# Attention-map scores contracted over 128 rows in a two-block transformer kernel, and FFN semaphores shared

## The reference

```python
h = rms_norm_2(x, norm_mix_pre_g[l])
proj = h @ w_in[l]
mq, mk, mv, dq, dk, dv, ga, gb = jnp.split(proj, split_at, axis=-1)
...
ya = moba_attention(moba_heads(mq), moba_heads(mk), moba_heads(mv), moba_slopes)
...
yb = diff_attention(dq[:, :, 0], dq[:, :, 1], dk[:, :, 0], dk[:, :, 1], dv, lam, diff_slopes)
...
def probs(q, k):
    qc = lax.dynamic_slice_in_dim(q, t0, QB, axis=2)
    logits = jnp.einsum('bhqd,bhkd->bhqk', qc, k).astype(jnp.float32) * scale + bias[None]
    return jax.nn.softmax(jnp.where(causal, logits, NEG), axis=-1)
a = probs(q1, k1) - lam * probs(q2, k2)
return jnp.einsum('bhqk,bhke->bhqe', a.astype(v.dtype), v)
```

## Time and profile before

| | |
|---|---|
| time, median of 3 runs | 1957.36 us (1955.51 to 1958.13) |
| the profiled execution's own time | 1958.78 us |
| its span, first to last instruction | 1957.1 us |
| TensorE matmul busy | 1916.0 us, 98% of the span |
| VectorE busy | 908.2 us, 46% |
| ScalarE busy | 705.5 us, 36% |
| GpSimd busy | 176.8 us, 9% |
| mean granted TensorE clock | 0.991 of full speed |
| read from HBM | 172.67 MB, 89 GB/s over the span |

### The profile page before, as it was taken

One profiled execution on the slowest core, in us unless ns is written; L12 is line 12 of the kernel. 1 busy time (PEld: TensorE's weight loads), 2 busy tenths in 40 slices (PEclk: granted clock), 3 DMA queues, 4 the chain that ended last, 5 costly groups with the idle time before them and its releaser, 6 DMA issues.

```text
span 1957.1 us, 24117 instructions
## 1 busy us (share of the span) xinstructions
PE 1916.0 (98%) x9630; PEld 1559.2 (80%) x9630; DVE 908.2 (46%) x1182; ACT 705.5 (36%) x957; POOL 176.8 (9%) x150
## 2 busy tenths in 40 slices
PE   8999999998999999999999999999999989999998
PEld 6888888887778898888888878777667868888887
DVE  6444432447685654644443246343546454444313
ACT  5222221354534443522222143334545453222212
POOL 2000000205330200200000032000000030000000
PEclk9999999999999999999999999999999989999999
DMA  5333322232214223333322222111212323333222
GB/s 162 97 96 97 96 97 94 99 108 66 66 44 151 86 87 108 86 104 89 103 90 104 89 89 87 65 65 44 69 61 86 94 57 93 101 92 101 90 104 75
DMA packets 213697, 175.79 MB, mean 90 GB/s; under 512 B 6565, under 2 KB 201210, under 8 KB 213626
## 3 DMA queue, kind: packets, MB, share of 16 engines
q1 hardware_dynamic: 212928, 174.74, 29.1%
q10 hardware_dynamic: 698, 0.05, 0.0%
HBM read 172.67 MB, written 2.10 MB: 89 GB/s over the span
## 4 chain that ended last, share of the span: by engine, by line
PE 88%; DVE 5%; ACT 3%; POOL 2%; issue 1%; DMA 1%; SPq 0%; DVEq 0%; POOLq 0%; ACTq 0%
PE bank L484 25%; PE bank L486 24%; PE bank L485 24%; PE bank L658 6%; PE bank L531 2%; PE bank L951 1%; PE bank L532 1%; PE bank L533 1%; ACT w_hi L1049 1%; PE bank L920 1%; DVE w_lo L1511 1%; DMA w_raw<-in_w_in 1%; PE bank L935 1%; DVE n_lo L1520 1%; POOL sum_squares L425 0%
## 5 line engine op out<-in xcount | busy, mean ns | idle before, releaser
L484 PE MATMUL bank<-n_hi,w_hi 128*128 128x512 f32 x1760 | 707.9, 402 | 18.0 <-DVE n_lo L1520 9.5
L1511 DVE TENSOR_TENSOR w_lo<-w_raw,w_hi 128x2048 fp32r<-128x2048 f32 x160 | 369.1, 2307 | 744.4 <-ACT w_hi L1049 744.3
L486 PE MATMUL bank<-n_hi,w_lo 128*128 128x512 f32 x1760 | 690.9, 393 | 0.0
L485 PE MATMUL bank<-n_lo,w_hi 128*128 128x512 f32 x1760 | 690.5, 392 | 0.0
L1049 ACT CAST w_hi<-w_raw 128x2048 fp32r<-128x2048 f32 x160 | 305.4, 1909 | 600.9 <-PE bank L486 519.0
L484 PEld LDWEIGHTS bank<-n_hi,w_hi 128*128 128x128 f32 x1760 | 333.4, 189 | 103.4 <-issue 24.0
L486 PEld LDWEIGHTS bank<-n_hi,w_lo 128*128 128x128 f32 x1760 | 333.2, 189 | 71.1
L485 PEld LDWEIGHTS bank<-n_lo,w_hi 128*128 128x128 f32 x1760 | 333.8, 190 | 68.2 <-issue 2.6
L425 POOL TENSOR_TENSOR sum_squares<-sum_squares,sq 128x512 f32<-128x512 f32 x42 | 65.9, 1569 | 927.4 <-ACT sq L1064 923.0
L484 PE MATMUL bank<-h_hi,w_hi 128*128 (+1 forms) x352 | 137.1, 390 | 0.2
L486 PE MATMUL bank<-h_hi,w_lo 128*128 (+1 forms) x352 | 136.9, 389 | 0.0
(11 more groups left out here) (306 smaller groups left out, 1953.7 us busy)
## 6 DMA issues: line engine op xcount, KB each, us to landing
w_raw<-in_w_in SPq DMA_DIRECT2D x68, 512.0 KB, 4.6
w_raw<-in_ffn_gate SPq DMA_DIRECT2D x44, 512.0 KB, 4.1
w_raw<-in_ffn_up SPq DMA_DIRECT2D x44, 512.0 KB, 5.2
w_raw<-in_ffn_down SPq DMA_DIRECT2D x44, 512.0 KB, 3.9
w_raw<-in_w_gate SPq DMA_DIRECT2D x22, 512.0 KB, 4.1
w_raw<-in_w_up SPq DMA_DIRECT2D x22, 512.0 KB, 5.2
w_raw<-in_w_down SPq DMA_DIRECT2D x22, 512.0 KB, 4.2
w_raw<-in_w_kv_mem SPq DMA_DIRECT2D x16, 512.0 KB, 4.4
```

What stands on the lines that cost most here:

```text
L484: pe.matmul(acc, w_hi, x_hi, start=start, stop=False)
L485: pe.matmul(acc, w_hi, x_lo, start=False, stop=False)
L486: return pe.matmul(acc, w_lo, x_hi, start=False, stop=stop)
L1511: dve.tensor_tensor(wlo[par][:, :], raw[par][:, :], whi[par][:, :].bitcast(F32), ALU.subtract).then_inc(w_lo_ready, 1)
```

## The change

1. The columns of `w_in_2` come in the order q, k, q, k for both kinds of attention, so that units 0 and 1 hold all that maps 0 to 3 need (`MIX2_COLS`, and the destinations in VectorE's turns).
2. For each map SyncE copies the 64 rows of its k and of its q inside SBUF, each twice, into the two halves of a 128-row tile (`map_kk`, `map_qq`; four transfers of 64 x 512 float32, 128 KB each; `load_pair`). The two pairs of tiles lie on the buffers `sq` and `tmp`.
3. ScalarE rounds both tiles to float32r (`pair_split`: `map_kk_hi`, and `map_q_hi_lo`, whose two halves then both hold the high part of q). VectorE subtracts: the low part of the doubled k (`map_kk_lo`), and the low part of q into the lower half of `map_q_hi_lo` alone (`pair_lo`).
4. A part of the scores is then two float32r matmuls over 128 rows, for all 16 maps: `map_q_hi_lo` by `map_kk_hi` (high q by high k plus low q by high k in one pass) and `map_q_hi_lo` by `map_kk_lo`. The eight high and eight low parts of the moba q and k, made in turns 0 to 3 before (L1426, L1976), are gone.
5. The 18 semaphores of the three FFNs become 6; the waits count on from one FFN to the next. In the second and third FFN the waits on them are the same waits with larger numbers.

```diff
-MIX2_COLS = [256 * j for j in range(MIX2_UNITS)]
+MIX2_COLS = [256 * j for j in (0, 2, 1, 3, 4, 5, 6, 8, 7, 9)] + [256 * j for j in range(10, MIX2_UNITS)]
...
+        sq_at = cursor[0]
         sq = [sb(f"sq{s}", [P, T], F32) for s in range(2)]
         tmp = [sb(f"tmp{s}", [P, T], F32) for s in range(2)]
+        kdup = [at(f"map_kk{s}", [P, T], F32, sq_at + 2048 * s) for s in range(2)]
+        kdl = [at(f"map_kk_lo{s}", [P, T], F32R, sq_at + 2048 * s) for s in range(2)]
+        qdup = [at(f"map_qq{s}", [P, T], F32, sq_at + 4096 + 2048 * s) for s in range(2)]
...
-        mql = at("moba_q_lo", [P, HEADS, T], F32R, arena + 16 * KB)
-        mkl = at("moba_k_lo", [P, HEADS, T], F32R, arena + 48 * KB)
-        mqh = at("moba_q_hi", [P, HEADS, T], F32R, arena)
-        mkh = at("moba_k_hi", [P, HEADS, T], F32R, arena + 8 * KB)
+        kdh = at("map_kk_hi", [P, T], F32R, arena + 92 * KB)
+        qst = at("map_q_hi_lo", [P, T], F32R, arena + 94 * KB)
...
-        ffn = [{k: sem(f"{k}_{f}") for k in ("gu_scaled", "silu_ready", "h_product", "h_hi_ready", "h_ready", "down_done")}
-               for f in range(3)]
+        gu_scaled, silu_ready, h_product = sem("gu_scaled"), sem("silu_ready"), sem("h_product")
+        h_hi_ready, h_ready, down_done = sem("h_hi_ready"), sem("h_ready"), sem("down_done")
...
+            def load_pair(m):
+
+                c, rows = (m % 8) // 2, slice(64 * (m % 2), 64 * (m % 2) + 64)
+                sp.wait_ge(m2_dve, 4 + 4 * (c // 2) + (8 if m >= 8 else 0))
+                if m >= 2:
+                    sp.wait_ge(map_scores, 4 * (m - 1))
+                for dst, src in ((kdup, mk if m < 8 else dk), (qdup, mq if m < 8 else dq)):
+                    for half in range(2):
+                        sp.dma_start(dst[m % 2][64 * half:64 * half + 64, :], src[rows, c, :]).then_inc(pair_loaded[m % 2], 16)
...
+                if j >= 5:
+                    load_pair(j - 5)
...
+                if MIX2_UNITS + j - 5 < MAPS:
+                    load_pair(MIX2_UNITS + j - 5)
...
-                s_ = ffn[f]
+                h0 = FC * f
...
-                        pe.wait_ge(s_["gu_scaled"], 2 * (j - 1))
+                        pe.wait_ge(gu_scaled, 2 * (j + (h0 - 1)))
...
-                c, rows = (m % 8) // 2, slice(64 * (m % 2), 64 * (m % 2) + 64)
                 if part == 0:
-                    if m < 8:
-                        pe.wait_ge(moba_ready, HEADS + c + 1)
-                    else:
-                        pe.wait_ge(*m2_emptied(8 + c // 2))
+                    pe.wait_ge(pair_ready, 2 * m + 2)
...
-                    if m < 8:
-                        mm = products(out_, mqh[rows, c, t0], mql[rows, c, t0], mkh[rows, c, s0], mkl[rows, c, s0], True, True)
-                    else:
-                        mm = pe.matmul(out_, dq[rows, c, t0], dk[rows, c, s0], start=True, stop=True)
-                    mm.then_inc(map_scores, 1)
+                    pe.matmul(out_, qst[:, t0], kdh[:, s0], start=True, stop=False)
+                    pe.matmul(out_, qst[:, t0], kdl[m % 2][:, s0], start=False, stop=True).then_inc(map_scores, 1)
...
+            def pair_split(m):
+                act.wait_ge(pair_loaded[m % 2], 64 * (m // 2 + 1))
+                if m:
+                    act.wait_ge(map_scores, 4 * m)
+                act.copy(kdh[:, :], kdup[m % 2][:, :]).then_inc(pair_hi, 1)
+                act.copy(qst[:, :], qdup[m % 2][:, :]).then_inc(pair_hi, 1)
...
-                        if v < 4:
-                            ch = 2 * (v % 2) + b
-                            act.wait_ge(m2_dve, 2 * v + b + 1)
-                            act.copy((mqh if v < 2 else mkh)[:, ch, :], (mq if v < 2 else mk)[:, ch, :]).then_inc(moba_hi, 1)
...
                 if has_out(v - 5) and v - 5 >= 8:
                     map_root((v - 5 - 9) // 2)
+                if 0 <= v - 2 < MAPS:
+                    pair_split(v - 2)
                 if has_out(v - 4):
                     map_copies(v - 4)
...
+            def pair_lo(m):
+                dve.wait_ge(pair_hi, 2 * m + 1)
+                dve.tensor_tensor(kdl[m % 2][:, :], kdup[m % 2][:, :], kdh[:, :].bitcast(F32), ALU.subtract).then_inc(pair_ready, 1)
+                dve.wait_ge(pair_hi, 2 * m + 2)
+                dve.tensor_tensor(qst[64:P, :], qdup[m % 2][64:P, :], qst[64:P, :].bitcast(F32), ALU.subtract).then_inc(pair_ready, 1)
...
-                        src, ch = bank[2 * (v % 2) + b][:, :], 2 * (v % 2) + b
-                        if v in (0, 1, 6, 7):
-                            dve.scalar_tensor_tensor((mq if v < 2 else dq)[:, ch, :], src, 64.0 ** -0.5, rstd[:, :],
+                        src, ch = bank[2 * (v % 2) + b][:, :], 2 * (v % 6 // 2) + b
+                        if v in (0, 2, 6, 8):
+                            dve.scalar_tensor_tensor((mq if v < 4 else dq)[:, ch, :], src, 64.0 ** -0.5, rstd[:, :],
                                                      ALU.mult, ALU.mult).then_inc(m2_dve, 1)
-                        elif v in (2, 3, 8, 9):
+                        elif v in (1, 3, 7, 9):
                             dve.tensor_tensor((mk if v < 4 else dk)[:, ch, :], src, rstd[:, :], ALU.mult).then_inc(m2_dve, 1)
...
-                    for b in range(2):
-                        ch = 2 * (v % 2) + b
-                        lo_, full, hi_ = (mql, mq, mqh) if v < 2 else (mkl, mk, mkh)
-                        dve.wait_ge(moba_hi, 2 * v + b + 1)
-                        dve.tensor_tensor(lo_[:, ch, :], full[:, ch, :], hi_[:, ch, :].bitcast(F32), ALU.subtract).then_inc(moba_ready, 1)
...
                     map_maxima(v - 3)
+                if 0 <= v - 2 < MAPS:
+                    pair_lo(v - 2)
```

More of the change, by code:

```diff
@@ L267, in two_blocks @@
         vm_hi, vm_ready, ptx_hi = sem("vm_hi"), sem("vm_ready"), sem("ptx_hi")
-        moba_hi, moba_ready = sem("moba_hi"), sem("moba_ready")
+        pair_loaded = [sem("pair_loaded0"), sem("pair_loaded1")]
+        pair_hi, pair_ready = sem("pair_hi"), sem("pair_ready")
         m2_act, m2_dve, m2_tanh = sem("m2_act"), sem("m2_dve"), sem("m2_tanh")
@@ L1095, in ffn_steps @@
             def ffn_steps(f, base):
-                s_ = ffn[f]
+                h0 = FC * f
                 def gate_up(par, half, j, jj):
                     split(par, half)
-                    act.wait_ge(s_["gu_scaled"], 2 * j + 1)
-                    act.activation(sq[jj][:, :], sq[jj][:, :], ACT.Silu).then_inc(s_["silu_ready"], 1)
+                    act.wait_ge(gu_scaled, 2 * j + (2 * h0 + 1))
+                    act.activation(sq[jj][:, :], sq[jj][:, :], ACT.Silu).then_inc(silu_ready, 1)
                     if f == 2 and isinstance(j, int) and j == 0:
@@ L1110, in gate_up @@
                         dst = hhi[:, bass.ds(j, 1), :].rearrange("p o t -> p (o t)")
-                    act.copy(dst, tmp[jj][:, :]).then_inc(s_["h_hi_ready"], 1)
+                    act.copy(dst, tmp[jj][:, :]).then_inc(h_hi_ready, 1)
                 def copy_turned(i, dst):
@@ L1493, in _ @@
                     else:
-                        act.wait_ge(ffn[2]["down_done"], i + 1)
+                        act.wait_ge(down_done, 2 * (C - 1) + i + 1)
                     if i:
@@ L1529, in add_down @@
                     if c < C - 1:
-                        dve.wait_ge(ffn[f]["down_done"], c + 1)
+                        dve.wait_ge(down_done, (C - 1) * f + c + 1)
                     else:
@@ L1562, in gate_up @@
                     if not first:
-                        dve.wait_ge(s_["h_ready"], j - 1)
-                    dve.tensor_tensor(sq[jj][:, :], bank[2 * jj][:, :], rstd[:, :], ALU.mult).then_inc(s_["gu_scaled"], 1)
-                    dve.tensor_tensor(tmp[jj][:, :], bank[2 * jj + 1][:, :], rstd[:, :], ALU.mult).then_inc(s_["gu_scaled"], 1)
-                    dve.wait_ge(s_["silu_ready"], j + 1)
-                    dve.wait_ge(s_["gu_scaled"], 2 * j + 2)
-                    dve.tensor_tensor(tmp[jj][:, :], sq[jj][:, :], tmp[jj][:, :], ALU.mult).then_inc(s_["h_product"], 1)
-                    dve.wait_ge(s_["h_hi_ready"], j + 1)
+                        dve.wait_ge(h_ready, j + (h0 - 1))
+                    dve.tensor_tensor(sq[jj][:, :], bank[2 * jj][:, :], rstd[:, :], ALU.mult).then_inc(gu_scaled, 1)
+                    dve.tensor_tensor(tmp[jj][:, :], bank[2 * jj + 1][:, :], rstd[:, :], ALU.mult).then_inc(gu_scaled, 1)
+                    dve.wait_ge(silu_ready, j + (h0 + 1))
+                    dve.wait_ge(gu_scaled, 2 * j + (2 * h0 + 2))
+                    dve.tensor_tensor(tmp[jj][:, :], sq[jj][:, :], tmp[jj][:, :], ALU.mult).then_inc(h_product, 1)
+                    dve.wait_ge(h_hi_ready, j + (h0 + 1))
                     if isinstance(j, int):
```

17 lines of the change are left out of this document (8 added, 9 removed).

## The result

| | before | after |
|---|---|---|
| time, median | 1957.28 us (1955.51 to 1958.13, 4 runs) | 1929.27 us (1928.36 to 1930.66, 4 runs) |
| the profiled execution's own time | 1958.78 us | 1929.94 us |
| its span | 1957.1 us | 1928.2 us |

The ratio is 0.9859 with a 95% interval of 0.9842 to 0.9876: 28.0 us faster, where 23.2 were forecast. The time lies 4.9 us under the forecast and 0.2 us under the lower end of the range. Timed again beside the first experiments the changed kernel took 1931.34 us, ratio 0.9863 (0.9846 to 0.9879).

A forecast was written before the change was run, and what follows sets the result against it. TensorE, busy 293.00 of 293.00 us in the stage, was taken as the bound. A gain of 26.2 us less 3.0 us of waits gave 23.2 us, so 1934.2 us from the 1957.36 us median; range 1929.5 to 1943 us.

The forecast's parts named there:

- The price after: TensorE's score products after the change: eight float32r matmuls over 128 rows, 1.22 us a map, bounds 1.16 and 1.28.
- The price of a score part before: TensorE between dense products: three parts sum to 2.72 us in map 3, 3.00 us in map 14.
- The change of form: TensorE going to 64-row products and back: 0.3 us in each of 48 score parts, 14 us of the gain.
- The two waits: TensorE at the second transposes of units 16 and 18, behind ScalarE's casts: about 1.5 us each, 3.0 us lost.
- The transfers: Copies of q and k inside SBUF land in 5 us, needed after 12.5 to 16 us, costing TensorE nothing.
- FFN semaphores: Sharing semaphores over the three FFNs costs nothing: same waits at the same places.
- The clock: TensorE's granted clock around the third FFN's start may shift: 2 us allowed either way.
- No waits: Rival: TensorE does not wait in units 16 and 18, 1931.2 us; chance 0.12.
- more waits than two: Rival: ScalarE's turn bounds all eight differential units, each losing 1.5 us, 1943 us; chance 0.12.
- late transfers: Rival: pairs land late at ScalarE's pair_split, holding back copies and transposes, about 1995 us; chance 0.03.
- weight loads that no longer hide: Rival: each new TensorE matmul waits 0.19 us for its weight load, 24 us back, 1958 us; chance 0.02.
- the cost of going over stays: Rival: TensorE's 0.3 us per score part is not the form's, 14 us gain lost, about 1948 us; chance 0.06.

The follow-up runs named there:

- e2: Changed kernel with its two score products a tile over rows 0 to 63 only, low q by high k left out: 1945.06 us, ratio 0.9935 to before.
- e9: Changed kernel, casts behind ScalarE's first copy to map_pt; in turns 15 and 17 that copy ahead of tanh, casts behind the second copy: 1928.17 us.
- e10: As e2, but a map's three score parts made one behind the other at the third place of its unit: 1937.50 us, ratio 0.9894 to before.
- e11: Changed kernel with a map's three score parts at the third place of its unit, over 128 rows, nothing left out: 1931.54 us.
- e7: Kernel before with only the six FFN semaphores shared over the three FFNs: 1958.06 us, ratio 1.0000 to before.
- e1: Changed kernel with ScalarE's two casts of a pair behind the first copy to map_pt of its turn, not ahead: 1928.63 us, ratio 0.9851 to before.
- e3: Changed kernel with a third score product a tile over 128 rows, the first one made twice: 1938.33 us, ratio 0.9902 to before.
- e5: Changed kernel with GpSimd's product of distance and slope waiting for VectorE's low parts of the next pair: 1929.85 us, ratio 0.9855 to before.

## Why the prediction was right, and which term was too small

- **The bound.** Right. TensorE's products were the whole stage, and what was taken off them came off the kernel. VectorE's pair of subtractions, "some 1.3 us", takes 1.8 in ten maps; that was covered.
- **The price after.** Right: 1.22 us a map forecast, 1.19 to 1.24 measured. This measure too ends one product too soon, by 0.05 us a map, 0.8 in all.
- **The price of a score part before.** This is the term that was too small. The prediction measured "from the last dense start before it to the first after it, less that 0.23", and that ends one product too soon. The change of form also made the first dense product behind the part 0.1 us late: 48 x 0.1 = 4.8 us. e2 shows it (0.38 us for an excursion, where 0.3 was taken), and e9, which has no wait, gives the gain on TensorE with everything in it: (255.21 - 226.03) / 15 x 16 = 31.1 us, for 26.2 forecast.
- **The change of form.** Right in kind: "more than half of the gain". It is 18.2 of 31.1 us, forecast as 14. The products that are left out are the rest: 8 x 0.67 = 5.4 us for the moba maps, and 8 x 0.96 = 7.7 for the float32 products; the three make 31.3 us for the 31.1. The Trainium skill's rule is that a change of tiling mode drains the engine (TensorEngine Tiling (Array Packing), Key Properties). The runs agree in that the price belongs to the change of form (e2, e10 and e11); that it is a drain, no view here shows.
- **The two waits.** Right in place, number, releaser and length: units 16 and 18, ScalarE's copy to `map_pt`, 1.47 us for 1.5. In time they cost 3.4 us, not the forecast's 3.0, by e9. Of the working for unit 18, tanh was to end 0.35 us before TensorE wants the copy (1451.85 and 1452.2) and ends 0.07 behind (1427.73, and 1427.43 + 0.23 = 1427.66); casts, copy and handover were to take 1.85 us and take 1.56. The two errors nearly cancel, which is luck.
- **The transfers.** Right: 5 us taken. The landing times after the change, of the k tiles and then of the q tiles:

```profile
DMA to landing us min/median/max: 3.9/4.8/5.5
DMA to landing us min/median/max: 3.7/4.6/6.2
```

- **FFN semaphores.** Right, nothing (e7). **The clock.** Within the 2 us allowed.
- **The sum.** 31.1 - 3.4 = 27.7 us, between the two measured gains of 28.0 and 26.5 us. With the 4.8 us counted as gain the forecast would have been 1929.4. The lower end of the range, "all of the gain with the clock in its favour", took no error in the price before, as if a measured distance had none. That is why it was missed by 0.2 us; the second timing, 1931.34 us, lies inside the range.
- **The rivals.** No waits, more waits than two, late transfers and weight loads that no longer hide: none shows in the trace after, where the new products follow each other at 0.23 us. That the cost of going over stays is refuted by e2 and e11 together.

## What to carry to other kernels

An excursion of TensorE from 128-row to 64-row products and back costs 0.38 us here with two or four products in it and 0.41 with eight, so short excursions are the dear ones: stack operands to the full height, or make all products of the other form in one go. Measure what a piece of work costs from landmark to landmark a whole unit apart, not from its own first to last row, since it can make its neighbours late. And work added to an engine that is idle on the mean is free only behind what the bound engine waits for. Here the two turns without slack cost 1.7 us each; putting the casts behind the copy took 1.05 of it back (e1), putting the copy ahead of tanh the rest (e9).

## What the runs showed of the hardware beyond what was expected

- A change of form makes two products late, 0.1 us each, in a stream of products of 0.23 us: the first and the second of the new form, on the way in and again on the way out (e2, e10).
- A wait costs more than its idle time says: 1.68 us for 1.47, and 0.3 us in e3 for none shown.
- A VectorE subtraction with both inputs in SBUF takes 0.44 us longer when GpSimd starts a product of a 128x512 tile at that moment: 1.12 and 0.69 us. The Trainium skill (SBUF — State Buffer, SBUF: two separate sides) has a lock between these two engines for such a pair, held for the whole instruction of the one that starts first. The kind agrees and the length doesn't: by its record, which is rough for GpSimd, the product lasts 1.49 us, but VectorE is held up only until about 0.46 us after its start (three distances, under e5). The next subtraction, which begins at 1368.89 while GpSimd runs until 1369.19, takes its usual 0.69.
- Sixteen transfers of 32 KB inside SBUF land in less time each than four of 128 KB: median 3.0 and 4.8 us for the k tiles, 1.9 and 4.6 for the q tiles. The sixteen come late by the time that their issues take, about 0.6 us each.
